# Recurrent mixer: output weights loaded in two blocks, half of the output projection interleaved with the last recurrence steps

## The reference, cut to what matters

```python
o = o * lax.rsqrt(jnp.mean(o * o, axis=-1, keepdims=True) + EPS) * gn_w
o = o.reshape(B, T, HG_VDIM) * jax.nn.silu(gate)
return o @ w_out, s_f, s_b          # (T,1024) @ (1024,1024), and the final states
...
xp = xp + g1p * op                   # residual, gate g1 from ada_w
hp = _rmsnorm(xp, norm2_w[l]) * (1 + sc2p) + sh2p
xp = xp + g2p * _moe(hp, ...)        # 64 routed experts and one shared expert
```

## Time and profile before

| | |
|---|---|
| time, median of 3 runs | 1507.22 µs (1505.87 to 1507.53) |
| profiled execution | 1505.39 µs, span 1503.6 µs |
| TensorE busy | 1464.5 µs, 97% of the span |
| VectorE, ScalarE busy | 468.9 µs, 436.9 µs |
| data moved | 510.50 MB, mean 340 GB/s |

### The profile page before, as it was taken

One profiled execution on the slowest core, in us unless ns is written; L12 is line 12 of the kernel. 1 busy time (PEld: TensorE's weight loads), 2 busy tenths in 40 slices (PEclk: granted clock), 3 DMA queues, 4 the chain that ended last, 5 costly groups with the idle time before them and its releaser, 6 DMA issues.

```text
span 1503.6 us, 26618 instructions
## 1 busy us (share of the span) xinstructions
PE 1464.5 (97%) x11057; PEld 861.0 (57%) x11057; DVE 468.9 (31%) x1002; ACT 436.9 (29%) x1088; POOL 3.2 (0%) x17
## 2 busy tenths in 40 slices
PE   5999999999999999999999999999999999999997
PEld 3868678554554545555456867654554545545454
DVE  2343452523222232222323151622223222222222
ACT  2133341323232232323222141323232232222323
POOL 0000000000000000000000000000000000000000
PEclk9999999999999999999999999999999999999999
DMA  9966679489999999999999417749999999999990
GB/s 334 370 225 232 231 283 375 197 346 397 407 401 410 389 420 388 418 399 395 416 404 279 177 77 288 272 188 395 410 400 408 393 413 406 397 403 405 410 392 33
DMA packets 101184, 510.50 MB, mean 340 GB/s; under 512 B 11120, under 2 KB 19600, under 8 KB 51984
## 3 DMA queue, kind: packets, MB, share of 16 engines
q1 hardware_dynamic: 97824, 507.05, 84.9%
q10 hardware_dynamic: 3312, 2.77, 0.5%
HBM read 506.65 MB, written 3.15 MB: 339 GB/s over the span
## 4 chain that ended last, share of the span: by engine, by line
PE 93%; SPq 2%; ACT 2%; DVE 1%; DMA 1%; issue 0%; DVEq 0%; ACTq 0%
PE psum L1333 91%; SPq L439 1%; PE psum L1667 1%; DMA arena<-in_hgrn_w_in 1%; SPq L396 1%; ACT arena L550 0%; DVE arena L862 0%; PE psum L1548 0%; PE psum L1792 0%; DVE arena L907 0%; ACT arena L573 0%; ACT L561 0%; PE psum L1848 0%; DVE arena L864 0%; PE psum L1461 0%
## 5 line engine op out<-in xcount | busy, mean ns | idle before, releaser
L1333 PE MATMUL psum<-arena 128*128 128x96 bf16 (+9 forms) x10772 | 1440.2, 368 | 18.5 <-DMA arena<-in_ada_w 5.3
L1333 PEld LDWEIGHTS psum<-arena 128*128 128x128 bf16 (+4 forms) x10772 | 835.9, 124 | 615.0 <-issue 522.9
L550 ACT ACTIVATE arena<-psum 128x192 f32<-128x192 f32 (+6 forms) x546 | 195.6, 385 | 371.1 <-PE psum L1333 312.8
L1216 DVE TENSOR_TENSOR arena<-psum,arena 128x512 f32<-128x512 f32 x124 | 85.2, 687 | 297.9 <-ACT arena L550 297.9
L1203 DVE SCALAR_TENSOR_TENSOR arena<-arena,psum 128x256 f32<-128x256 f32 x64 | 43.2, 675 | 254.3 <-ACT arena L713 254.3
L550 ACT ACTIVATE arena<-arena 128x512 bf16<-128x512 f32 (+2 forms) x140 | 86.3, 625 | 107.9 <-DVE arena L1216 105.5
L1220 DVE TENSOR_TENSOR arena<-arena 128x512 bf16<-128x512 f32 x124 | 85.8, 692 | 95.1 <-ACT arena L550 95.1
L713 ACT ACTIVATE arena<-psum 128x256 f32<-128x256 f32 x64 | 24.6, 385 | 295.8 <-PE psum L1333 295.8
L1192 DVE COPY arena<-psum 128x192 f32<-128x192 f32 x128 | 39.8, 352 | 82.2 <-PE psum L1333 82.2
L907 DVE SCALAR_TENSOR_TENSOR arena<-psum,arena 128x128 f32<-128x128 f32 x64 | 17.5, 343 | 56.7 <-PE psum L1333 56.7
L557 ACT ACTIVATE arena<-arena 128x512 f32<-128x512 f32 x16 | 9.8, 628 | 62.7 <-DVE arena L907 61.7
(11 more groups left out here) (157 smaller groups left out, 305.7 us busy)
## 6 DMA issues: line engine op xcount, KB each, us to landing
arena<-in_moe_w_gate SPq DMA_DIRECT2D x64, 2048.0 KB, 9.6
arena<-in_moe_w_up SPq DMA_DIRECT2D x64, 2048.0 KB, 14.1
arena<-in_moe_w_down SPq DMA_DIRECT2D x64, 2048.0 KB, 11.1
arena<-in_ada_w SPq DMA_DIRECT2D x24, 2048.0 KB, 12.7
arena<-in_hgrn_w_in SPq DMA_DIRECT2D x10, 2048.0 KB, 12.9
arena<-in_na_w_qkv SPq DMA_DIRECT2D x6, 2048.0 KB, 13.4
arena<-in_hgrn_w_out SPq DMA_DIRECT2D x1, 4096.0 KB, 14.0
arena<-in_na_w_o SPq DMA_DIRECT2D x1, 4096.0 KB, 13.6
```

What stands on the lines that cost most here:

```text
L550: return act.activation(out, in_, ACT.Copy, **kw)
L1216: dve.tensor_tensor(y_rest[:, at], psum[:, 6 + half, :], y[:, j, 0, at], ALU.subtract)\
L1333: return pe.matmul(out, lhsT, rhs, start=start, stop=stop, skip_group_check=True, **kw)
```

## The change

The output weights become two blocks of the staged series, `("out", 0)` and `("out", 1)`, 2 MB each, heads 0 to 3 and heads 4 to 7, in rooms 3 and 4 (the two halves of `late`). They are loaded before the last three `ada_w` blocks, which now go to rooms 0 to 2. TensorE's last two rounds are written out: the first part of the projection is cut into four pieces of two k each, which stand before item 4, before `ada(14)`, before item 5 and before `ada(15)`. The second part follows item 6. Layer 1 uses the same function with the same order as before.

```diff
+        late_halves = [late[:, 4 * n:4 * n + 4].rearrange("p h (c n) -> p h c n", c=2) for n in range(2)]
...
         stages0 = len(stages)
+        stages += [("out", half) for half in range(2)]
...
-        qkv0 = stages0 + 6
+        qkv0 = stages0 + 8
...
-        rooms = [(n - stages0 + 3) % 5 for n in range(stages0)] + [5, 6, 3, 4, 0, 1, 2, 3, 4, 0, 1, 2, 7, 8]
+        rooms = [(n - stages0 + 11) % 5 for n in range(stages0 - 3)] + [0, 1, 2] + [3, 4] + [5, 6, 3, 4, 0, 1, 2, 3, 4, 0, 1, 2, 7, 8]
...
-            for n in range(5, stages0):
+            for n in range(5, stages0 - 3):
                 sp.wait_ge(*block_used(n - 5))
                 load_stage(n)
-            for n in (stages0 - 5, stages0 - 4):
-                sp.wait_ge(*block_used(n))
-            sp.dma_start(late, io["hgrn_w_out"][0].rearrange("(h p) d -> p h d", p=P)).then_inc(late_in, 16)
+            for half in range(2):
+                sp.wait_ge(*block_used(stages0 - 8 + half))
+                load_stage(stages0 + half)
+            for n in range(3):
+                sp.wait_ge(*block_used(stages0 - 6 + n))
+                load_stage(stages0 - 3 + n)
             for n in range(stages0 - 3, stages0):
                 sp.wait_ge(*block_used(n))
             sp.wait_ge(qk_done, 16)
-            load_stage(stages0)
-            load_stage(stages0 + 1)
+            load_stage(stages0 + 2)
+            load_stage(stages0 + 3)
             load_gate_up(0, 0, 0)
             load_down(0, 0, 0)
             sp.wait_ge(late_half, 1)
             load_shared_gate_up(0)
             sp.wait_ge(out_ps, 4)
             load_shared_down(0)
-            sp.wait_ge(*block_used(stages0 + 1))
+            sp.wait_ge(*block_used(stages0 + 3))
...
-                if b is not None:
-                    project(b, KINDS[b % 5] == "v", midway, norm=0 if b == 0 else None)
-                else:
-                    midway()
+                if b is None:
+                    break
+                project(b, KINDS[b % 5] == "v", midway, norm=0 if b == 0 else None)
...
+            out_weights(0)
+            pe.wait_ge(o_done, 1)
+            pe.wait_ge(unit_free[0], 5)
+            pe.wait_ge(unit_free[1], 5)
+            out_half(0, 0, oT, range(0, 2))
+            recur(1, 4)
+            out_half(0, 0, oT, range(2, 4))
+            ada(14)
+            out_half(0, 0, oT, range(4, 6))
+            recur(1, 5)
+            out_half(0, 0, oT, range(6, 8))
+            ada(15)
+            recur(1, 6)
+            out_weights(1)
+            pe.wait_ge(o_done, 2)
+            out_half(0, 1, oT)
+            at_stage[0] = stages0 + 2
...
-            project_out(1, oTa, [(oa_sb, 3)], [(oa_sb, 4)])
+            pe.wait_ge(late_in, 16)
+            pe.wait_ge(oa_sb, 3)
+            out_half(1, 0, oTa)
+            pe.wait_ge(oa_sb, 4)
+            out_half(1, 1, oTa)
```

More of the change, by code:

```diff
@@ L331, in stage_source @@
                 return rows[:, half * (K // 2):(half + 1) * (K // 2)]
+            elif what[0] == "out":
+                rows = io["hgrn_w_out"][0, what[1] * BLOCK:(what[1] + 1) * BLOCK]
+                return rows.rearrange("(h p) (c n) -> p h c n", p=P, c=2)
             elif what[0] == "in":
@@ L344, in block_used @@
         def block_used(n):
-            ada_n = sum(w[0] == "ada" for w in stages[:n + 1])
-            return (ada_ps, ada_n) if stages[n][0] == "ada" else (proj, n + 1 - ada_n)
+            kinds = [w[0] for w in stages[:n + 1]]
+            if kinds[-1] in ("ada",):
+                return ada_ps, sum(w in ("ada",) for w in kinds)
+            return proj, sum(w in ("in", "qkv") for w in kinds)
         SMALL, ROUTE = 5 * 16, 5 * 16
@@ L395, in load_stage @@
                 room = (stage_ada if stages[n][0] == "ada" else stage)[rooms[n]]
+                if stages[n][0] == "out":
+                    room = late_halves[stages[n][1]]
                 sp.dma_start(room, stage_source(stages[n])).then_inc(stage_in[room_sem[n]], 16)
@@ L1514, in _ @@
                     ada(n)
[L1516 to L1533, removed]
-                        ins.then_inc(late_half, 1)
-                for i in range(2, 4):
-                    norm_sum(2 * m + 1, i)
@@ L1538, in _, with out_half @@
-            project_out(0, oT, [(o_done, 2), (unit_free[0], 5), (unit_free[1], 5)])
+            def out_half(m, part, src, ks=range(K)):
+                for k in ks:
+                    for h in range(part * K // 2, (part + 1) * K // 2):
+                        ins = mm(psum[:, k // 2, (k % 2) * NT:(k % 2 + 1) * NT], late[:, h, k * P:(k + 1) * P], src[:, h],
+                                 h == 0 and k % 2 == 0, h == K - 1)
+                    if part == 1 and k % 2:
+                        ins.then_inc(out_ps, 1)
+                        if k >= 5:
+                            norm_sum(2 * m + 1, k // 2 - 2)
+                    if part == 0 and k == K - 1:
+                        ins.then_inc(late_half, 1)
+                if part == 1:
+                    for i in range(2, 4):
+                        norm_sum(2 * m + 1, i)
@@ new lines, in out_weights @@
+            def out_weights(half):
+                n = stages0 + half
+                pe.wait_ge(stage_in[room_sem[n]], 16 * room_count[n])
+            out_weights(0)
[9 more added lines that the diff above has]
+            out_half(0, 0, oT, range(6, 8))
```

## The result

The change makes the kernel slower: 1515.54 µs (median of 4 runs, 1514.68 to 1516.73) against 1506.55 before (1505.86 to 1507.53, 4 runs), ratio 1.0059, interval 1.0047 to 1.0071, that is 7.1 to 10.7 µs. I had forecast slower by 4.9 µs, range up to 1515.0. The direction and the place were right, the size was too small.

The account below looks back on a forecast made before the run. The prediction took the kernel as a TensorE chain with small holes; the 5.5 µs gain is swallowed by a shared-weights wait, +3.2, plus half clock, +1.7: +4.9 on 1507.2, 1512.1 µs, range 1507.5 to 1515 for 8 in 10.

Parts of the forecast that it names:

- Rival B: At the shared expert's wait: shared weights land in time, gain stays, -5.5 to -2.0 µs, about 1503.5; chance 0.09.
- Rival D: State store before `norm_sum(1, 0)`: lands behind 12.6 MB of loads, at about 270, +17 µs; chance 0.03.
- Rival C: At the shared expert's wait: weights land at 270 to 272, clock dips once, 0 to +3 µs, 1509.1; chance 0.15.
- new landing: Shared weights' landing before the shared expert: 262.9 + 12.8, less 1.3 pause and 0.9 store, giving 273.5.
- The start of the burst: SP's loads queued behind `ada(15)`: start at 236.6 instead of 223.80, 12.8 µs later.
- The stream: Loads from SP's burst to the shared weights' landing: from 236.6 to 273.5.
- the pause before the shared down weights: DMA queue run dry between 258.2 and 259.5, waiting for `out_ps`; 1.3 µs to be saved.
- shared weights, behind the old start: TensorE's start of `shared`: at 273.5 after a hole of up to 8.7 µs, 3.2 µs behind the old kernel.
- half clock behind the hole: TensorE after the shared-weights hole: one stretch at half clock, 1.7 µs, between 0 and 3.4.
- the gain that the hole swallows: TensorE before the shared expert: 5.5 µs from holes (3.0), half clock (1.7) and drains (0.8).
- 0.8 µs for drains: TensorE after `ada(13)`: pipeline drains ahead of the filled holes, 0.8 of the 5.5 µs gain.
- the late landing: Shared weights land at 274.8 if the pause is not saved; +4.5 µs in the upper bound of +7.9.

Follow-up runs that it names:

- e1: New loads of the changed kernel kept, TensorE put back in the old order; 1506.89 µs, ratio 0.9996 to the kernel before.
- e6: Changed kernel with ScalarE's wait for the state stores moved behind the norm; 1516.24 µs, ratio 1.0056 to the kernel before.
- e5: Changed kernel plus nine useless matmuls ahead of the wait for the shared weights; 1512.99 µs, ratio 1.0040 to the kernel before.
- e3: Changed kernel with TensorE reordered so `ada(15)` follows `ada(14)` directly, behind one piece instead of four; 1503.18 µs, ratio 0.9975 to the kernel before.
- e7: Changed kernel with `ada(16)`, `ada(17)` blocks issued ahead of SP's waits and ScalarE's store wait behind the norm; 1503.43 µs, ratio 0.9970 to the kernel before.
- e4: Changed kernel, layer 0's shared down weights on their own semaphore, waited for only in `shared_down`; 1512.83 µs, ratio 1.0034 to the kernel before.
- e2: Changed kernel with SP issuing the `ada(16)` and `ada(17)` blocks before waiting for those of `ada(13)` to `ada(15)`; 1510.56 µs, ratio 1.0023 to the kernel before.
- e8: Changed kernel with `ada(15)` moved ahead of item 5 and piece four; 1510.41 µs, ratio 1.0022 to the kernel before.

## Why the prediction was wrong in size

**The mechanism** was right, step by step. The pieces cover ScalarE's chain and hold the clock; the early loads cost nothing that can be measured (e1); `ada(15)` moves behind all pieces and SP's next burst with it; the shared weights are the new wait and swallow what was gained before it (e6); the clock falls in and behind the hole (e5).

Rival B (shared weights in time) needed a stream of 490 GB/s. The trace shows 424 between 254 and 266 µs and 352 between 267 and 272, where the packets of shared gate and up (1024 B) pass. Rival D (store behind all loads) did not occur: 11.0 µs to landing. Rival C had the landing between 270 and 272; it came at 276.1 on the clock of the old profile.

The Trainium skill's page "DMA: Bandwidth & Descriptors" (section "Anatomy of one DMA — SWDGE (gpsimd) path") gives 2.0 µs plus bytes over 436 GB/s for one transfer issued from GpSimd. The prediction's estimate from it for this stream, nine transfers issued by SP and ScalarE, was 33.9 µs. Measured were 277.9 - 239.3 = 38.6: the figure does not carry over to this stream.

**The step that failed** is the term "new landing" of the shared weights. On the clock of the old profile it came at 277.96 - 1.8 = 276.1, and I had put it at 273.5 (and the end of the hole at 273 to 275). Both of its parts were too small:

- The start of the burst: 236.6 forecast, 239.3 - 1.8 = 237.5 measured, 0.9 late. From the end of `ada(13)` TensorE needed 21.5 µs, where my sum of undrained prices gave 20.8: piece four took 3.6 µs (233.53 to 237.16) instead of 3.5, the others about the same, and item 5 0.75 (232.78 to 233.53) instead of 0.4. The other 0.2 are the way from the end of `ada(15)` to the issue (223.6 to 223.80 before), which I had left out.
- The stream: 36.9 µs forecast, 38.6 measured. I had subtracted 1.3 µs for the pause before the shared down weights. It was no pause in the DMA engine that finished last, as these rows of the kernel before show:

```profile
243.37 7.64 SPq L409 DMA_DIRECT2D arena<-in_shared_w_up  x1
```
```profile
arena<-in_shared_w_up SPq DMA_DIRECT2D x1, 1024.0 KB, 17.0
```

Shared up landed at 243.37 + 17.0 = 260.4, 2 µs behind the time when the mean rate fell, and shared down 2.5 µs behind it (262.9). In the changed kernel, with a queue that never ran dry, down landed 2.5 µs behind up as well (277.9 and 275.4): the pause had cost nothing, so nothing could be saved. A landing is the end of a load's last packet, and a mean over 16 engines does not show it. I had written 274.8 as the bound for this case and should have taken it as the value. The stream's last 0.4 µs have no single cause that I can show.

| | forecast | measured |
|---|---|---|
| shared weights, behind the old start | +3.2 | +5.8 |
| half clock behind the hole | +1.7 | +1.8 |
| sum | +4.9 | +7.6 |
| medians | | +9.0 (7.1 to 10.7) |

The half clock was sized well. So was the gain that the hole swallows, nearly: 5.5 forecast, 4.9 in e3 and 4.5 in e7 where nothing swallows it. The 0.8 µs for drains in it was the rest of a difference, and no run shows it by itself.

**What is left open.** The last 1.4 µs lie within the interval. The rest of the span, from the SiLU on, took between 1225.3 and 1228.4 µs in the ten profiles, 1226.3 in that of the kernel before and 1228.0 in that of the changed one. A part of this is an unexplained wait of TensorE behind the first expert loop, 2.19 µs in the old profile, 3.26 in the new, and 2.4 to 2.7 in e1 to e4, so it varies from run to run. The 1.8 µs taken off at the start are less clear. The nine profiles with the new loads all have `ada(13)` 1.4 to 3.4 µs later than the one profile of the kernel before. But over these nine kernels the ratio, in µs, differs from the change of the stretch by -0.7 to +1.6, 0.5 in the mean, so most of the late start does not show in the times. I have no run that ties the rest to the change.

**The range** was too narrow above. Its top was the late landing and two stretches at half clock, +4.5 + 3.4; the start of the burst, a sum of eight prices, had no bound of its own, nor had the tail of the slowest DMA engine.

## What to carry to other kernels

When work is moved ahead of an instruction, look for the queue that waits for that instruction's count: 13.6 MB of loads stood behind `ada(15)`, and starting them 13.7 µs later (237.5 against 223.8) cost more than the holes that were filled. Run first the steps that release transfers (e3), or take the loads that need not wait out from behind the wait (e7). Two holes in a row on one engine don't add up: the first is worth nothing while the second waits for something independent (e6), and the same edit pays once the second is gone (e7). And moving one load earlier can make another transfer later: ask what it will meet (e2, e8).

## What the runs showed of the hardware

- A transfer's landing depends on what it shares the engines with, even from another queue. The state store of 256 KB took 11.0 µs to land beside packets of 4096 B (the changed kernel), 12.8 and 13.5 with 4096 B at first and 8192 B later (e3, e8), 14.9 and 15.1 beside 8192 B throughout (e2, e7), and 2.3 with hardly any load beside it (the forward state of the changed kernel). The Trainium skill's page "DMA: Bandwidth & Descriptors", section "Queues, rings and completion order", says that each engine takes turns between queues, a packet each. The traces agree in the main: in e2 the store's 512 packets passed among 499 of the other queue's, of 8192 B, in 10.3 µs; in the changed kernel among 610 of 4096 B, in 6.7 µs.
- A hole costs its length and then the clock. Two kernels whose wait ended at the same 277.96, one idle before it for 8.2 µs and one kept busy, differ by 1.79 µs in the next marked step. The store's hole of 1.95 µs in the changed kernel left the clock at 1.00; one of 5.9 µs (e2) did not.
